# Delta rule: the rows of summed gates spread by DMA from a DRAM scratch in place of products on TensorE

## The reference, cut to what matters

```python
gc = jnp.cumsum(logg, axis=-1)
decay = jnp.exp(jnp.where(tril, gc[..., :, None] - gc[..., None, :], -jnp.inf))
m = jnp.eye(CHUNK) + jnp.where(strict, jnp.einsum('bhcid,bhcjd->bhcij', kb, k) * decay, 0.0)
rhs = jnp.concatenate([v * beta[..., None], kb * jnp.exp(gc)[..., None]], axis=-1)
sol = lax.linalg.triangular_solve(m, rhs, left_side=True, lower=True, unit_diagonal=True)
aqk = jnp.einsum('bhcid,bhcjd->bhcij', q, k) * decay
qg = q * jnp.exp(gc)[..., None]
```

## Time and profile before

| what | value |
|---|---|
| median of 3 runs | 2189.33 us (2188.45 to 2189.74) |
| profiled execution, span from first to last instruction | 2185.7 us |
| profiled execution's own time around the span | not given apart; the median is 3.6 us above the span |
| TensorE busy | 1882.4 us, 86% of the span |
| VectorE, ScalarE, POOL busy | 804.4, 507.6, 335.2 us |
| mean granted clock of TensorE | 0.958 |
| spread products L1053 | 32 records for 16 products |

### The profile page before, as it was taken

How to read it: one execution, slowest core, us unless ns; L and a number is a source line. 1 busy time by engine, 2 the same in 40 slices (tenths; PEclk the granted TensorE clock), 3 DMA queues, 4 the chain that set the end, 5 groups by cost and what they waited for, 6 DMA issues and landing times.

```text
span 2185.7 us, 32921 instructions
## 1 busy us (share of the span) xinstructions
PE 1882.4 (86%) x14024; PEld 1132.1 (52%) x14024; DVE 804.4 (37%) x1427; ACT 507.6 (23%) x1119; POOL 335.2 (15%) x323
## 2 busy tenths in 40 slices
PE   6999889999999998888889999989999975666565
PEld 3874668745875433333236556677787731212112
DVE  3331757555633010000026877566774300000001
ACT  2452321343012100001023323444442100000001
POOL 1431054322320000000013000054540000000000
PEclk9999999999999999999999999999999998878888
DMA  9321031240239999999993433200004699999997
GB/s 385 142 86 73 5 118 78 119 190 1 89 150 384 428 430 426 429 431 431 428 407 147 169 154 140 103 2 2 2 2 174 233 428 429 430 427 432 430 430 298
DMA packets 46689, 528.07 MB, mean 242 GB/s; under 512 B 3408, under 2 KB 7760, under 8 KB 23120
## 3 DMA queue, kind: packets, MB, share of 16 engines
q1 hardware_dynamic: 44784, 522.56, 57.3%
q10 hardware_dynamic: 1760, 3.42, 0.4%
HBM read 524.91 MB, written 1.05 MB: 241 GB/s over the span
## 4 chain that ended last, share of the span: by engine, by line
PE 53%; DMA 28%; DVE 12%; issue 2%; ACT 2%; DVEq 1%; PEld 1%; PEldq 0%; POOLq 0%; POOL 0%; ACTq 0%; SPq 0%
DMA ring<-in_moe_w 27%; PE bank L1435 12%; PE bank L709 8%; PE bank L820 7%; PE bank L1317 4%; PE bank L1250 3%; PE bank L788 3%; DVE ring L2421 2%; DVE x L2280 2%; PE bank L1036 2%; PE bank L1013 2%; DVE x L2859 1%; PE bank L961 1%; DMA ring<-in_mod_w 1%; PE bank L627 1%
## 5 line engine op out<-in xcount | busy, mean ns | idle before, releaser
L1435 PE MATMUL bank<-ring,xgs 128*32 128x512 f32 x2984 | 374.0, 655 | 129.4 <-DMA ring<-in_moe_w 128.0
L1435 PEld LDWEIGHTS bank<-ring,xgs 128*32 128x32 f32 x2984 | 106.3, 119 | 370.6 <-issue 284.9
L1435 PE MATMUL bank<-ring,hT 128*32 128x512 f32 x1488 | 190.1, 663 | 75.3 <-DMA ring<-in_moe_w 75.1
L820 PE MATMUL bank<-hT,ring 128*128 128x256 f32 (+1 forms) x784 | 232.7, 454 | 2.0 <-ACT hT L1607 1.4
L2700 DVE SCALAR_TENSOR_TENSOR x<-bank,modT,x 128x256 f32<-128x256 f32 x96 | 42.4, 480 | 457.1 <-PE bank L1461 456.9
L820 PEld LDWEIGHTS bank<-hT,ring 128*128 128x128 f32 x784 | 146.6, 190 | 82.3 <-issue 66.8
L1435 PEld LDWEIGHTS bank<-ring,hT 128*32 128x32 f32 x1488 | 52.3, 120 | 199.3 <-issue 152.6
L2280 DVE SCALAR_TENSOR_TENSOR x<-gluR,cols,x 128x256 f32<-128x256 f32 x240 | 116.2, 484 | 16.6 <-issue 0.9
L709 PE MATMUL bank<-hT,ring 128*128 128x256 f32 x432 | 99.9, 381 | 3.7 <-ACT ssd_g L1658 2.2
L709 PEld LDWEIGHTS bank<-hT,ring 128*128 128x128 f32 x432 | 81.1, 190 | 17.9 <-issue 6.2
L3091 POOL MEMSET gluR<- 128x3008 f32 x1 | 2.6, 2610 | 498.9 <-DVEq L2710 498.9
(11 more groups left out here) (573 smaller groups left out, 3026.0 us busy)
## 6 DMA issues: line engine op xcount, KB each, us to landing
ring<-in_moe_w SPq DMA_DIRECT2D x56, 4096.0 KB, 22.8
ring<-in_moe_w SPq DMA_DIRECT2D x28, 2048.0 KB, 21.1
ring<-in_moe_w SPq DMA_DIRECT2D x55, 1024.0 KB, 14.4
ring<-in_mod_w SPq DMA_DIRECT2D x12, 4096.0 KB, 13.4
ring<-in_moe_w SPq DMA_DIRECT2D x12, 3072.0 KB, 22.0
ring<-in_cd_w SPq DMA_DIRECT2D x6, 4096.0 KB, 14.1
ring<-in_ab_w SPq DMA_DIRECT2D x5, 4096.0 KB, 15.3
ring<-in_ab_wo SPq DMA_DIRECT2D x2, 4096.0 KB, 14.9
```

The lines of the kernel that those rows point to most:

```text
L820: last = mm(ps[p["no"] % 4][:, p["c0"]:T], w[:, k, :], hT[:, k, p["c0"]:T], start=(k == 0), stop=(k == KD - 1))
L1435: last = mm(ps[banks + s][32 * j:32 * j + 32, :], lhs[s][:, 4 * kh + k, 32 * j:32 * j + 32], piece(g, k, j), start=(kh == 0 and k == 0), s ...
```

## The change

The 16 spread products and their semaphore `gdn_spr` go. SP has a new step, `decay_rows`, between the last "cdout" load and `load_experts` of layer 1. It writes the 64 rows of `small` to a DRAM scratch, waits for that, waits until the buffers are free, and then for every head issues two transfers, each of which reads one row of 2 KB from the scratch into all 128 partitions of one half of `ES[n % 2]`. From head 2 on it waits for the sixth `level_r` of head n - 2. ScalarE's `decay` waits for the head's two rows and works in place; the queries' exponential now comes before the last two tiles are overwritten, with a further drain. `turn_keys` takes over the waits of `spread` for the banks and no longer waits for `gdn_E`. Two other waits of TensorE are taken out, `gla_zeroed` and `routed`.

```diff
+        gate_rows = nc.dram_tensor("gate_rows", (64, T), F32, kind="Internal").ap()
...
+        def decay_rows(sp):
+
+            sp.wait_ge(sg("gate_cums"), 2)
+            sp.dma_start(gate_rows, small[0:64, :]).then_inc(sg("gate_rows_out"), 16)
+            sp.wait_ge(sg("gate_rows_out"), 16)
+            sp.wait_ge(sg("conf_ready"), 1)
+            sp.wait_ge(sg("proj_evacuated"), counts["tile"])
+            for n in range(KD):
+                if n >= 2:
+                    sp.wait_ge(sg("gdn_R"), 6 * (n - 1))
+                for d in range(2):
+                    sp.dma_start(ES[n % 2][:, d, :, :].rearrange("p t c -> p (t c)"),
+                                 gate_rows[n + 32 * d:n + 32 * d + 1, :].broadcast_to([P, T])).then_inc(sg(f"gdn_row{n % 2}"), 16)
...
                     if i == 0:
+                        if stage == "moe1":
+                            decay_rows(sp)
                         load_experts(sp, n, int(stage[3]))
...
-                def spread(n, d):
+                def turn_keys(n, d):
 
                     if n >= KD:
                         return
+                    if n == 0:
+                        keep_warm((10, 3)[d], 0)
+                    pe.wait_ge(sg("gdn_Kt"), 2 * n + 1)
                     if n > 0:
                         if d == 0:
                             pe.wait_ge(sg("gdn_S"), 2 * n)
                         else:
                             pe.wait_ge(sg("gdn_aqk"), n)
-                    mm(ps[4 + d], ident[:, n + 32 * d:n + 32 * d + 1].broadcast_to([P, P]), gcb,
-                       start=True, stop=True).then_inc(sg("gdn_spr"), 1)
-
-                def turn_keys(n, d):
-
-                    if n >= KD:
-                        return
-                    if n == 0:
-                        keep_warm((10, 3)[d], 0)
-                    pe.wait_ge(sg("gdn_Kt"), 2 * n + 1)
-                    pe.wait_ge(sg("gdn_E"), 2 * n + d + 1)
...
-                    spread(n, 0)
...
-                    spread(n, 1)
...
-                    act.wait_ge(sg("gdn_spr"), 2 * n + d + 1)
+                    act.wait_ge(sg(f"gdn_row{n % 2}"), 32 * (n // 2 + 1))
                     e = ES[n % 2][:, d, :, :]
                     for t in range(NT):
-                        A_(e[:, t, :], ps[4 + d][:, t * P:t * P + P], ACT.Abs, bias=ngcT[:, t, d, n:n + 1])
-                    A_(qcs[n % 3][:, 256 * d:256 * d + 256], ps[4 + d][:, SEQ:T], ACT.Exp)
+                        if t == 2:
+                            A_(qcs[n % 3][:, 256 * d:256 * d + 256].rearrange("p (t c) -> p t c", t=2), e[:, 2:4, :], ACT.Exp)
+                            act.drain()
+                        A_(e[:, t, :], e[:, t, :], ACT.Abs, bias=ngcT[:, t, d, n:n + 1])
                     act.drain()
                     A_(e, e, ACT.Exp, scale=-1.0).then_inc(sg("gdn_E"), 1)
```

More of the change, by code:

```diff
@@ L1062, in turn_keys @@
                     pe.wait_ge(sg("gdn_Kt"), 2 * n + 1)
-                    pe.wait_ge(sg("gdn_E"), 2 * n + d + 1)
+                    if n > 0:
+                        if d == 0:
+                            pe.wait_ge(sg("gdn_S"), 2 * n)
+                        else:
+                            pe.wait_ge(sg("gdn_aqk"), n)
                     for t in range(NT):
@@ L1452, in scatter @@
                     done = Q * layer + q
-                    if q == 0 and steps[0] == 0:
-                        pe.wait_ge(sg("routed"), layer + 1)
                     for dt in steps:
@@ L1545, in _ @@
             project_gla()
-            pe.wait_ge(sg("gla_zeroed"), 1)
             pe.wait_ge(sg("proj_evacuated"), copied(GLA_PAIRS, 0))
@@ L2181, in gla_begin @@
                 V.memset(attm[:, :, :, :], 0.0)
-                dve.drain().then_inc(sg("gla_zeroed"), 1)
+                dve.drain()
                 dve.wait_ge(sg("gla_gz"), 2 * GH)
@@ L2680, in route @@
                         V.tensor_copy(gateT[:, s, 2 * half:2 * half + 2, :], ps[5 + half][:, :].rearrange("p (q t) -> p q t", q=2)).then_inc(sg("gates_copied"), 1)
-                dve.drain().then_inc(sg("routed"), 1)
+                dve.drain()
             def experts(layer, streams):
```

## The result

The changed kernel takes 2208.65 us, median of four runs (2206.39 to 2209.76), against 2188.89 us for the kernel before in four runs (2186.19 to 2189.74). The ratio is 1.0087, with a 95% interval of 1.0073 to 1.0100: slower by 0.87%, 16 to 22 us. The forecast was 2209.4 us. The runs after also give a time and a span for the same execution (2209.76 and 2208.0 us, 1.8 us apart), so the profiled execution of before, with its span of 2185.7, took about 2187.5 us, 1.8 us less than the median on which I had put the sum.

What follows compares the result with a forecast made beforehand. TensorE, 86% busy, looked binding, but engines take turns at the delta rule's start and VectorE holds the head turns' chain first. 9.7 + 2.0 + 8.4 = +20.1 us on the 2189.3 median gave 2209.4 us, range 2198 to 2216.

Steps and rivals of the forecast that it cites:

- Products, gain 0: Start and head turns: the sixteen removed TensorE products are hidden, at the turns by VectorE; gain 0.
- The rival in which the change is faster: Turns and start: removed products are on the path, 0.8 us a turn plus 1.1 us, -6.9 us, 2182.4; chance 4%.
- Queue at the start, +9.7: Delta rule start: the write waits behind a 4096 KB load, then rows transfer; first decay +9.7 us (9.2 to 10.3).
- My middle between 2.9 and 4.0: Start: time for head 0's row transfers to land, taken as 3.4 us between a store and a small broadcast.
- Clock at the start, +2.0: Delta rule start: after about 12 us of TensorE waiting, key products run at half rate; +2.0 us (0 to 2.5).
- Clock at the turns, +8.4: Seven head turns: without spread products TensorE's clock falls, 1.2 us each; +8.4 us (0 to 12).
- The first rival: Head turns: the clock holds, so only the start counts; 2201.0 us; chance 30%.
- SP at the other heads, 0: Heads 1 to 7: row transfers arrive in time, with up to 7.3 us from L1017's end costing nothing; 0 us.
- ScalarE would wait for nothing new: Head turns, a sign in the profile after: ScalarE has no new waits there; no size given.
- The rival of late rows: Six heads' turns: rows come later than 7.3 us after L1017, 2.3 us each, +14 us on top, 2223; chance 6%.
- ScalarE, 0: ScalarE's decays read SBUF in place with one more drain each; 0 to 0.7 us, taken as 0.
- the removed waits, 0: TensorE's waits on zeroed GLA states and routing: neither appears among the releasers, so removing them gives 0 us.

Runs made afterwards that it cites:

- the control: Kernel before plus small warming products at head 0's sixth level and nine behind the second turn's first spread product: 2189.92 us, ratio 1.0003.

## Why the prediction was right, step by step

The forecast of 2209.4 us met 2208.65, and +20.1 stood against 19 to 20 us. Every term had its sign and its mechanism, but two of them were off in opposite directions, by +1.7 and -2.7 us, so that the total came within 1 us is in part luck.

**Products, gain 0: right.** No turn after is shorter than the 28.7 us of before, and VectorE's stretch from the last level's copy (L2415, 1518.31) to the first of the next head's levels by the same line (1527.20, ending at 1527.85) is 9.5 us long, as the earlier trace rows had it. The rival in which the change is faster rested on that stretch ending with L1036. It falls, but for its first product: the start without it is worth 1.6 to 1.9 us, where I had said 1.1. (That rival's sum, 7 x 0.8 and 1.1 us, is 6.7 us and not the 6.9 that I gave.)

**Queue at the start, +9.7: right in kind, too small by 1.7 us.** Measured +11.42, above the 9.2 to 10.3 that I had given it. The write landed behind the load, as said, and the load took 13.9 us here, not the 12.9 of the earlier trace rows, which the two kernels without a write show to be the short one: with issues, 14.1 us from the load to the rows' issue, where I had 13.3. The pair of rows took 4.3 us behind its first issue, 4.7 with it, where I had 3.9 with both issues. My middle between 2.9 and 4.0 was the wrong choice: the small broadcast is the nearer row in form as well, and the second row took 4.3 us from its issue. By the estimate from the Trainium skill, "DMA: Bandwidth & Descriptors", section "Anatomy of one DMA", the pair would land 3.2 us after its first issue. That section's figures are for transfers that POOL issues, and these are SP's; alone on the engines, in the kernel with early rows, the pair landed 4.6 us after its first issue, so here the measurement decides. The slow completion of a write to HBM that the section warns of is not to be seen: the write was there within 0.3 us of the load's end, though the load may have covered a part of it.

**Clock at the start, +2.0: right, with 0.3 us that is not the clock's.** +1.97 up to the first level: the key products took 3.53 us instead of 2.07, and 0.5 us lies ahead of them, half of it on the transposes at half rate (0.66 us, where the kernel with early rows has 0.41). In the two kernels in which the clock is 1.00 there, early rows and warming at the start, it is 10.14 us from the first decay to the first level, against 9.88 before: 0.26 us of the +1.97 are not the clock's, and 1.71 us are. But warming them gave nothing in the end, since the clock fell one step later. The term was a real cost and not one to be recovered alone.

**Clock at the turns, +8.4: right in kind, too large by 2.7 us.** Measured +5.75, within 0 to 12. I had charged all seven turns with 1.2 us. The clock was low in four. At the fifth and sixth, for 3.4 us each, that cost 1.35 and 1.4 us; at the third, for 6.8 us, 2.4 us; at the second, twice for 3.4 us, 0.6 us against a turn that already held a low stretch before, which is less than that turn differs by between the traces of this case with all products in place (30.36 and 32.19 us). At the first, fourth and seventh nothing was lost. The price of a fall was good (1.35 for 1.2), the count was not. The products put back bring all turns behind the second to 28.7 or 29.1 us and the clock to 1.00, which shows the cause.

The first rival, that the clock would hold at the turns, is refuted. It leant on 1.85 us busy at 1446.4; after, 1.16 us busy was followed by a fall. By the rule of the Trainium skill, "TensorE: Matmul & The Clock Gate", section "HAM oscillation — how this bites in real kernels", the clock would have held through idle pieces as short as these 3.2 us; the trace disagrees.

**SP at the other heads, 0: right.** The rows came 5.2 us behind L1034, where I had 3.9, with the bound at 7.3, and made late to 7.3 they cost 0.4 us in six turns. ScalarE is held by them for 0.2 to 0.7 us at three turns in the kernel after, as in this row of ScalarE's timeline, and it costs nothing:

```profile
1493.18 0.69 ACT L1811 ACTIVATE hT<-hT,gts 128x128 f32<-128x128 f32 x2 [0.68 <-DMA hT<-gate_rows]
```

So my sentence that ScalarE would wait for nothing new was wrong, and the number beside it right. The rival of late rows would have come true with rows somewhere between 2.1 and 4.3 us later than they came.

**ScalarE, 0, and the removed waits, 0: right,** the first within its bounds, with the 0.26 us above at the start; the second, within 2 us, by a run of its own.

Still open: why it is the third, fifth and sixth turn that grow, and the same ones in five kernels that have no products at the turns (the kernel after, the two with early transfers, the one with warming at the start, and the one with rows at 7.3 us), while the fourth and seventh do not. The clock tells which turns they are; what decides it was not tried.

## What to carry to other kernels

A small transfer paid for what stood ahead of it on its queue: 128 KB took 13.7 us behind 4096 KB. Before a step is moved to a DMA queue, look for the last big load that it will stand behind, and issue it ahead of that, with its buffers' waits.

Products on TensorE that lay in another engine's stretch cost nothing here, and they were what held the clock. When such work is taken out, sum TensorE's busy time in the stretch that stays, compare it with stretches of the same trace that were followed by a fall, and charge the fall to the work behind it, not to the gap. Here this told that the clock would fall, and not at which turns. A low clock repaired at one place can come back at the next, so a repair is judged by the whole stage.

## What was not expected of the hardware

- Transfers that spread one row of 2 KB over 128 partitions (256 KB each) moved only 165 to 200 GB/s in a pair with nothing else under way, where the 4096 KB loads of the same queue move about 430.
- What a low clock costs depends on whose work lies under it: 3.4 us of it at the second turn of the kernel before cost nothing that the control could show, as much at the fifth turn after cost 1.35 us, and 6.8 us at the third 2.4 us.
- Products with 64 x 64 tiles keep TensorE busy in the profile and did not hold the clock ahead of the fall at 1443.0. Two products of 128x512 at each turn held it behind the second turn, two of 128x128 at the same places did not.
- The second turn differs between traces with the same work in it: 30.36 us in the kernel before, where the clock was low from 1443.0 to 1446.4, and 32.19 in that kernel without the two waits, where it was low from 1443.8 to 1454.0. The medians of the two kernels agree within 0.1%; that the waits have no part in it is not shown.
